# RWKV pairs: root transposes ahead of the increments, turned keys and a piece of weights between the states, the two decay products back to back

## The reference

```python
w = -softplus(-(w0 + tanh(wd) @ w2)) - 0.5
decay = exp(-exp(w))
a = sigmoid(a0 + ad @ a2)
kk = kk / max(sqrt(sum(kk * kk)), 1e-12)
k = k * (1.0 + (a - 1.0) * k_a)
aa = -kk
bb = kk * a4
def step(state, inp):
    sa = einsum('bhij,bhj->bhi', state, a_t)
    state = state * w_t + sa * b_t + v_t * k_t
    return state, einsum('bhij,bhj->bhi', state, r_t)
y = (y - mean) * rsqrt(var + RWKV_GN_EPS) * ln_w + ln_b
```

## Time and profile before

| | |
|---|---|
| median of three runs | 3329.46 us (3325.09 to 3331.16) |
| profiled execution | 3329.62 us |
| its span | 3327.8 us |
| PE busy | 3242.5 us, 97% of the span |
| PE weight loads busy | 2664.4 us, 80% |
| DVE, ACT, POOL busy | 53%, 37%, 6% |
| DMA | 97 GB/s on average |

### The profile page before, as it was taken

One profiled execution on the slowest core, in us unless ns is written; L12 is line 12 of the kernel. 1 busy time (PEld: TensorE's weight loads), 2 busy tenths in 40 slices (PEclk: granted clock), 3 DMA queues, 4 the chain that ended last, 5 costly groups with the idle time before them and its releaser, 6 DMA issues. The chain is left out here.

```text
span 3327.8 us, 52710 instructions
## 1 busy us (share of the span) xinstructions
PE 3242.5 (97%) x22179; PEld 2664.4 (80%) x22179; DVE 1774.2 (53%) x2970; ACT 1247.7 (37%) x1967; POOL 193.2 (6%) x156
## 2 busy tenths in 40 slices
PE   7999999999999999989999999999999999999999
PEld 6877777777777787867788888888888888888887
DVE  5235555545555455363436777433656566655832
ACT  4124343433333332242325666323334344443421
POOL 1000000001001111100000111010000000000000
PEclk9999999999999999999999999999999999999999
DMA  7433333331212134332442122443332233322552
GB/s 234 114 82 87 86 98 92 87 109 48 62 54 83 57 113 146 95 114 76 111 110 80 45 58 86 130 145 108 89 89 89 76 95 94 96 89 76 165 143 85
DMA packets 492528, 324.30 MB, mean 97 GB/s; under 512 B 27130, under 2 KB 448605, under 8 KB 491782
## 3 DMA queue, kind: packets, MB, share of 16 engines
q1 hardware_dynamic: 492294, 320.94, 33.3%
HBM read 276.05 MB, written 44.85 MB: 96 GB/s over the span
## 5 line engine op out<-in xcount | busy, mean ns | idle before, releaser
L534 PE MATMUL PS<-XH,WHT 128*128 128x512 f32 (+1 forms) x2224 | 897.7, 404 | 7.1 <-DVE AR L1031 2.1
L522 DVE TENSOR_TENSOR WLT<-AR,WHT 128x1024 fp32r<-128x1024 f32 (+1 forms) x430 | 527.3, 1231 | 667.2 <-ACT WHT L516 666.8
L536 PE MATMUL PS<-XH,WLT 128*128 128x512 f32 (+1 forms) x2224 | 872.6, 392 | 0.0
L516 ACT ACTIVATE WHT<-AR 128x1024 fp32r<-128x1024 f32 (+1 forms) x430 | 446.9, 1042 | 646.6 <-PE PS L536 483.5
L535 PE MATMUL PS<-XL,WHT 128*128 128x512 f32 (+1 forms) x1712 | 671.2, 392 | 0.0
L534 PEld LDWEIGHTS PS<-XH,WHT 128*128 128x128 f32 (+1 forms) x2224 | 417.5, 188 | 109.2 <-issue 10.8
L536 PEld LDWEIGHTS PS<-XH,WLT 128*128 128x128 f32 (+1 forms) x2224 | 417.7, 188 | 96.2
L535 PE MATMUL PS<-ARR,WHT 128*128 128x512 f32 x1024 | 404.6, 395 | 0.0
L535 PEld LDWEIGHTS PS<-XL,WHT 128*128 128x128 f32 (+1 forms) x1712 | 321.7, 188 | 71.7 <-issue 4.6
L535 PEld LDWEIGHTS PS<-ARR,WHT 128*128 128x128 f32 x1024 | 192.4, 188 | 40.4 <-issue 0.2
L534 PE MATMUL PS<-XL,WHT 128*128 128x512 f32 x512 | 203.3, 397 | 0.1
(11 more groups left out here) (487 smaller groups left out, 5336.5 us busy)
## 6 DMA issues: line engine op xcount, KB each, us to landing
AR<-b_w_in SPq DMA_DIRECT2D x128, 512.0 KB, 4.0
AR<-w_in SPq DMA_DIRECT2D x122, 512.0 KB, 4.1
AR<-a_w_in SPq DMA_DIRECT2D x48, 512.0 KB, 4.4
AR<-w_out SPq DMA_DIRECT2D x32, 512.0 KB, 4.8
AR<-a_w_out SPq DMA_DIRECT2D x32, 512.0 KB, 4.0
AR<-b_w_out SPq DMA_DIRECT2D x32, 512.0 KB, 4.1
proj_scratch<-AR SPq DMA_DIRECT2D x33, 256.0 KB, 2.0
AR<-a_w_kv_up SPq DMA_DIRECT2D x32, 256.0 KB, 3.7
```

The source lines that it names most:

```text
L516: self.nc.scalar.activation(self.shaped(self.high, n), self.shaped(self.raw, n), ACT.Copy).then_inc(self.s_high, 1)
L522: self.nc.vector.tensor_tensor(self.shaped(self.low, n), self.shaped(self.raw, n), f32(self.shaped(self.high, n)), ALU.subtract).then_inc( ...
L534: mm(out, wh, xh[k0 + c], start=(start and c == 0), stop=False)
L536: last = mm(out, wl, xh[k0 + c], start=False, stop=(stop and c == nk - 1))
```

## The change

Nothing is added or taken from the arithmetic. (1) The two decay products stand next to each other after level 2, the second into bank 7. (2) In the tail of PE, the root transposes come before the increments, the first state before the products of y, piece 7 and the turned keys between states. (3) ACT writes rb first and does its high split of weights after the exponentials. (4) DVE does kn, yn and the rates before the state inputs, hb and qt are apart, and the low split comes last.

```diff
@@ -1415,19 +1415,20 @@
                 else:
-                    N.wait(pe, i, "act.sgw")
-                N.did(mm(B[6][:, :], W2[rows(e), :], TW[rows(e), :], start=True, stop=True), "pe", ("zw", "za")[e])
+                    E.wait(pe, i - 2, "act.yc")
+                    N.wait(pe, i - 1, "dve.bon")
+                N.did(mm(B[6 + e][:, :], W2[rows(e), :], TW[rows(e), :], start=True, stop=True), "pe", ("zw", "za")[e])
...
             def key_sums(i):
                 N.wait(pe, i, "act.sqk")
                 if i:
-                    N.wait(pe, i, "act.sga")
+                    N.wait(pe, i, "act.sgw")
...
             def key_roots(i):
-                N.wait(pe, i, "act.rb")
+                N.wait(pe, i, "act.rb", "act.sga")
@@ -1494,6 +1495,8 @@
             def value_scores(i):
                 N.wait(pe, i, "act.tokV")
                 N.wait(pe, i, "dve.bon")
+                if i + 1 < NPAIR:
+                    N.wait(pe, i + 1, "act.sga")
@@ -1569,8 +1574,8 @@
             ahead(1)
             decays(0, 0)
+            decays(0, 1)
             ahead(2)
-            decays(0, 1)
@@ -1603,33 +1608,36 @@
-                    if l in (2, 3) and more:
-                        decays(i + 1, l - 2)
+                    if l == 2 and more:
+                        decays(i + 1, 0)
+                        decays(i + 1, 1)
...
                 solved(i)
                 piece(i, 6)
-                increments(i)
-                outputs(i)
-                state(i, 1)
+                if more:
+                    key_roots(i + 1)
                 if tail:
                     out_roots(i - 1)
-                if more:
-                    key_roots(i + 1)
+                increments(i)
+                queries_solved(i)
+                state(i, 1)
+                outputs(i)
                 state(i, 2)
                 if more:
                     values_turned(i + 1)
                 state(i, 3)
+                piece(i, 7)
                 state(i, 4)
                 if more:
                     bs_turned(i + 1)
                 state(i, 5)
-                state(i, 6)
-                piece(i, 7)
                 if more:
                     ks_turned(i + 1)
+                state(i, 6)
+                if more:
                     as_turned(i + 1)
                 from_state(i)
@@ -1791,12 +1799,14 @@
-                split(i, 3)
+                if more:
+                    spread(i + 1)
                 if tail:
                     out_spread(i - 1)
                 if more:
-                    spread(i + 1)
                     exps(i + 1)
+                split(i, 3)
+                if more:
                     token_major(i + 1, V_, "V")
@@ -2041,34 +2058,40 @@
                     key_recip(i + 1)
                     scan(i + 1)
-                state_inputs(i)
-                split(i, 3)
-                state(i, 1)
-                if tail:
-                    out_normed(i - 1)
-                state(i, 2)
                 if more:
                     unit_keys(i + 1)
                 if tail:
-                    out_bonus(i - 1)
-                state(i, 3)
+                    out_normed(i - 1)
                 if more:
                     rates(i + 1)
-                state(i, 4)
+                state_inputs(i)
+                if more:
+                    decayed_rates(i + 1)
+                bare_states(i)
+                if tail:
+                    out_bonus(i - 1)
+                state(i, 1)
                 if tail:
                     out_gated(i - 1)
                 if more:
                     scaled_keys(i + 1)
+                state(i, 2)
+                if more:
+                    decayed_keys(i + 1)
+                state(i, 3)
+                if more:
+                    removals(i + 1)
+                state(i, 4)
+                state_queries(i)
+                if more:
+                    queries(i + 1)
                 state(i, 5)
                 if more:
-                    decayed_keys(i + 1)
-                    removals(i + 1)
+                    bonus(i + 1)
                 state(i, 6)
-                if more:
-                    queries(i + 1)
-                    bonus(i + 1)
                 if tail:
                     low(i - 1)
+                split(i, 3)
                 evac(tile(i, 1))
```

More of the change, by code:

```diff
@@ L1221, in rwkv @@
               pool=[f"lot{l}" for l in levels],
-              pe=[f"{x}{h}{l}" for l in levels[:-1] for x in "xt" for h in halves] + ["uv"] + [f"{x}{h}{NL - 1}" for x in "xt" for h in halves] + ["pt0", "pt1", "gt0", "h0", "gt1", "h1", "q", "y"] + [f"s{c}" for c in range(1, NCH - 1)] + ["yf"],
+              pe=[f"{x}{h}{l}" for l in levels[:-1] for x in "xt" for h in halves] + ["uv"] + [f"{x}{h}{NL - 1}" for x in "xt" for h in halves] + ["pt0", "pt1", "gt0", "h0", "gt1", "h1", "q", "s1", "y"] + [f"s{c}" for c in range(2, NCH - 1)] + ["yf"],
               act=[f"xc{h}{l}" for l in levels for h in halves] + ["uvc", "ptc0", "ptc1"],
-              dve=[f"ta{h}{l}" for l in levels for h in halves] + ["gti", "hb", "qt"] + [f"su{c}" for c in range(1, NCH - 1)])
+              dve=[f"ta{h}{l}" for l in levels for h in halves] + ["gti", "hb"] + [f"su{c}" for c in range(1, 5)] + ["qt"] + [f"su{c}" for c in range(5, NCH - 1)])
     E = Marks(k, "rwkvy", pe=["cen", "var", "vt"], act=["yy", "sqy", "yc", "vsqrt", "vb", "xh"], dve=["ve", "vrec", "yn", "yb", "yz", "xl"])
@@ L1519, in increments, with queries_solved @@
                     S.did(both(cs, one), "pe", f"h{h}")
+            def queries_solved(i):
+                S.did(each(range(NCH), lambda c, e: mm(B[0][rows(e), tok(c)], P1TA[rows(e), c, 1, :], GB[rows(e), c, 1, :], start=True, stop=True)), "pe", "q")
             def outputs(i):
-                S.did(each(range(NCH), lambda c, e: mm(B[0][rows(e), tok(c)], P1TA[rows(e), c, 1, :], GB[rows(e), c, 1, :], start=True, stop=True)), "pe", "q")
                 E.wait(pe, i - 1, "dve.ve")
@@ L1662, in gates @@
                     N.wait(act, i, "pe.za")
-                    N.did(A(AS, B[6][:, :], ACT.Sigmoid, bias=k.prm("a0", i)), "act", "sga")
+                    N.did(A(AS, B[7][:, :], ACT.Sigmoid, bias=k.prm("a0", i)), "act", "sga")
             def split(i, j):
@@ L1869, in rates, with decayed_rates @@
                 N.did(TTn(SQN, KK, AS, ALU.mult), "dve", "ba")
+            def decayed_rates(i):
                 N.wait(dve, i, "dve.ba", "act.ewi")
@@ L1932, in state_inputs, with bare_states @@
                 S.did(TTn(GTI, B[2][:, :].rearrange("p (c f) -> p c f", f=CH), eye(NCH), ALU.add), "dve", "gti")
+            def bare_states(i):
                 S.wait(dve, i, "pe.h1")
@@ L1936, in state_inputs, with state_queries @@
                 S.did(TTn(HB, B[3][:, :].rearrange("p (c f) -> p c f", f=CH), WC2[i % 2].unsqueeze(2).broadcast_to([P, NCH, CH]), ALU.mult), "dve", "hb")
+            def state_queries(i):
                 S.wait(dve, i, "pe.q")
@@ L2006, in _ @@
             rates(0)
+            decayed_rates(0)
             scaled_keys(0)
```

## The result

The changed kernel takes 3297.08 us (median of four runs, 3295.54 to 3298.23); the kernel before, run on the same chip beside it, 3330.31 (3325.09 to 3338.04). The ratio is 0.9898 with an interval of 0.9878 to 0.9918: about 33 us less by the medians. The profiled execution took 3298.23 with a span of 3296.4, which is 31.4 less than the span before. Forecast were 3304.5, 25.15 us less, in a range from 3297 to 3314. The direction and the place are right, the size is too small.

A forecast was written before the change was run, and what follows sets the result against it. PE, busy 97% of the span, was taken as the bound, with open waits in the pairs' tails. 17.4 + 3.4 + 1.1 - 0.8 + 2.85 + 1.2 = 25.15 us from 3329.62 gave 3304.5 us, range 3297 to 3314.

The forecast's parts named there:

- the tail's four waits on PE: Tails of pairs 0 to 5: waits before turned values, fourth state, turned b and sixth state, 2.93 us together, would go.
- the new one: Tail, ahead of the first state: PE would newly wait 0.34 us for hb, which waits for bt on DVE.
- The decays: Ahead of level 3: two decay products side by side take 1.05 to 1.1 us; pairs 1 to 5 keep 0.26 each.
- the decays aren't staggered: Rival at the decay products: staggered, about 1.6 us, total 3308.7; 8 in 100 together with the serial case, 3313.
- DVE doesn't bound the tail: Rival in the tail: DVE becomes its bound, each pair loses 1 to 2 us, 3310 to 3316; 9 in 100.
- rb isn't late: Slower rival: key roots wait for a late rb and hold up all behind; with 4.6 us, 3336; 2 in 100.
- the size of the tail: Tails of pairs 0 to 5: each would gain 2.9 us, 17.4 us over six pairs.
- The step-by-step clock of the prediction: Tail of pair 2, timed step by step from differences of successive starts: `from_state` at 931.05 instead of 933.96.
- a third of its slow stretch: Tail of pair 6: half clock would last 6.8 us instead of 10.2, giving back 1.2 of 3.5 us lost.
- the two ends named: Pair 6: one slow stretch more or less (2.3 to 3.5 us), its 1.5 us of unexplained wait gone or not.
- The 0.8 us that the forecast takes off for it: Pair 7: out roots hold up increments for 1.3 us, hb costs 0.35, y gives 0.8 back: -0.8 us.
- The term itself: Levels and prologue, from the decay products: 5 x 0.26 + 2 x 1.05 = 3.4 us.

The follow-up runs named there:

- decays_undone: Changed kernel with the decay products put back, one ahead of level 3 and one ahead of level 4, in one bank: 3298.98 us, ratio 0.9903.
- decays_alone: Kernel before with only the two decay products side by side after level 2, in two banks: 3327.99 us, ratio 0.9984.
- evac_first: Changed kernel with DVE's evacuation of the projection's bank at level 3 ahead of the two steps mixing the keys: 3290.02 us, ratio 0.9878.
- piece7_old: Changed kernel with piece 7 and the turned keys back at their old place, piece 7 behind the sixth state: 3307.84 us, ratio 0.9919.
- best: Changed kernel with evacuation first except in pair 6, hb ahead of bt, and increments ahead of the roots in pairs 6 and 7: 3288.21 us, ratio 0.986.
- roots_behind: Changed kernel with the roots behind the first state on PE, and gti, hb and the first addition ahead of kn on DVE: 3304.38 us, ratio 0.9908.
- before_again: The kernel before, unchanged, profiled once more in one execution: 3337.49 us.
- back_later: Kernel before with pair 6's 1 MB transfer of `XL` issued after the products of y: 3329.36 us, ratio 0.9997.
- both best ones: `best`, and the same kernel with pair 6's first megabyte transfer started after the products of y: 3288.45 us, ratio 0.9855 for the latter.

## What of the prediction held, and the steps that failed

**What held.** What bounds the kernel: the tail's four waits on PE. All four are gone, and the new one is there, 0.30 us for 0.34. `decays_undone` shows that the reordered tails alone give nearly everything. Rb comes in time in pairs 0 to 5. Put_bonus and the Gram products don't slip: the Gram products of two pairs wait 0.83 us as before. The decays: a pair of them in 1.06 us; 0.26 us kept per pair, the rest a wait ahead of piece 4 (0.72 for some 0.8), shown by `decays_alone`, and its cause, the order on DVE, by `evac_first`. Pairs 6 and 7 wait 1.20 us for the roots (forecast 1.25 and 1.3), and pair 6 0.39 ahead of its fourth state. The tail of pair 5 is at full clock, worth 2.9 us for 2.85. Of the rivals none came: the decays aren't staggered, DVE doesn't bound the tail, and rb isn't late.

Which of the moves in the tail fills which wait is shown in part. Piece 7 between the states is worth 1.6 us a pair (`piece7_old`), hb ahead of bt another 0.27 (`best`), and the roots' place ahead of the increments nothing that can be seen (`roots_behind`). That the waits ahead of the turned values and the turned b went because DVE does kn and the rates earlier follows from the rows; no run puts these steps of DVE, or ACT's order, back alone.

**The step that failed: the size of the tail.** "It is the 2.93 of the waits, less 0.34, and some 0.3": 2.9 us a pair. Measured are 3.6. The brackets that make up the 2.93 begin at the modelled end of the work before, and that lies later than the time at which PE could have gone on. By successive starts the four intervals were 1.46 (second state to values turned), 0.69 (third to fourth state), 1.37 (fourth state to b turned) and 0.69 (fifth to sixth state), 4.21 us. Behind the same four states the next work now starts after 0.12, 0.21, 0.16 and 0.11, 0.60 in all. So the waits were worth 3.61, not 2.93, 0.17 more for each. Less the 0.30 that are new, 3.3 remain; roots and piece 6 are 0.07 shorter each, and the first and the sixth state, next to other work than before, 0.15 together.

The step-by-step clock of the prediction has the same fault from the other side: it put 0.21 to 0.25 for a state, read off a place where 128-row work follows. In the row a state now takes 0.11 to 0.16 where 64-row work follows, five times, and 0.21 ahead of piece 7. The Trainium skill, "Perfetto Trace Analysis", section "Summary: the profiler window per engine type", says that TensorE's records have an estimated end; the trace agrees, with the 0.17 us. `piece7_old` shows it independently: 1.32 us of brackets, 1.6 us of tail. Over six pairs this is 4 us of the 6 that were missed.

**The second step: pair 6.** Forecast were 1.1 for the waits and 1.2 for a third of its slow stretch; the tail gave 6.7. By the executions this splits up: `before_again`, at full clock and with 0.98 of stall, has 19.41, so with the 1.51 of the profiled one it would be 19.94, and its slow stretch cost 3.2 us. All of it went. The stall went too, 1.5 us; PE comes to that place later now, as it waits 1.20 us for the roots first, and the block of code (told at the end) is in by then. The remaining 2.0 are the waits, where 1.1 was forecast: the 3.6 of the other pairs, less the new 1.20 and 0.39. That I left this pair a slow stretch and the stall was the wrong choice between the two ends named.

**Pair 7.** The 0.8 us that the forecast takes off for it are there: from `solved` to `from_state` it takes 13.32 us for 12.52. But the profile of before has a slow stretch of 3.4 us right behind, at 1252.2, and that of the changed kernel has none there; the part from `from_state` on is 1.5 us shorter by it. All four profiles with the old tails have a stretch at this place, and two of the six with filled ones. Whether the change had a part in it is open, and the forecast had no term for it.

**What was taken back.** Levels and prologue gave 1.4 us in place of 3.4. The term itself holds: pairs 1, 3, 4 and 5 have -0.23 to -0.28, pair 6 -1.0, the prologue 1.2 by the key sums. But the two slow stretches of 3.4 us in the windows above cost some 2.6 together (against them stands 0.45 that pair 2 of the profiled kernel before took longer than its neighbours). Neither can be laid to the change alone. In the prologue `before_again` and `decays_undone` have a stretch of 6.8 us at the same place, all eight profiles with both decays together one of 3.4, and the first profile of the kernel before and `back_later` none. The one in pair 2 follows the new 0.72 us in both profiles of the changed kernel, one follows it in pair 5 of `piece7_old`, and none in `decays_alone` and `roots_behind`, which have that wait in five pairs each. `decays_undone` and `evac_first`, without it, have none in the levels.

**How far one profile carries.** The kernel before spreads from 3324.8 to 3338.4 us over 23 runs on one chip, the changed one over 3 and 5 us in four runs each, but `evac_first` and `best`, with tails filled as well, over 8 and 11. The four profiles with the old tails (the kernel before twice, `back_later`, `decays_alone`) show three to five of eight tails at half clock for 3.4 to 10.2 us, in other pairs each time but for pairs 5 and 7, and each costs 1.4 to 3.2. In the six profiles with filled tails (the changed one twice, `decays_undone`, `evac_first`, both best ones) none of pairs 0 to 6 has one in its tail. So filling the waits was worth more than their length. That the waits, and not something that goes with them, let the clock fall is only borne out by these ten. `piece7_old` speaks against waits as such: it puts two of them back in each of pairs 0 to 6, 0.39 and 0.93 us, and none of its tails is at half clock. Which waits it takes stays open.

## What to carry to other kernels

Price a wait on TensorE by the difference of successive starts with and without it, not by its bracket: here each of four waits was worth some 0.17 us more than it showed. Where short products with waits between them sit beside stretches at half clock, count the stretches over several profiles before you decide what filling the waits is worth, as they move from run to run. And when work moves up, see what the bank it needs hangs on: here two operations in front of an evacuation took back 0.8 of 1.05 us in each of five pairs, and turning them round gave 5 us in the rows, 7 by the medians, which are of two chips. See too what covers each step in the pairs that lack a piece of work: an order on DVE that cost nothing in six pairs cost PE 2.84 us in the seventh.

## What the runs showed of the hardware

- **Half clock after little waiting.** In the old tails, where PE waits 0.38 to 1.14 us at four places between products of 64 rows, the granted clock fell to 0.50 in three to five of eight tails per profile. In `piece7_old`, with 0.39 and 0.93 us per tail, it fell in none. In pair 2 of the changed kernel it fell right behind a single wait of 0.72 us, in both of its profiles.
- **A wait for code.** PE stopped for 0.90 to 1.59 us in pair 6 in four profiles (the kernel before twice, `decays_alone`, `best`), each time until 1.3 to 1.5 us after a 16 KB block of the queue "instruction" landed. The block came in at the end of SP's 1 MB transfer into `XL` and landed 0.3 to 0.9 us after the last of it. With the transfer issued later the stop is gone in both kernels that tried it (the kernel before and the best one). The Trainium skill, "Runtime: NRT & Kernel Launch", section "Instruction fetch mechanics", says that engines load their program in blocks of 16 KiB on a queue of their own, and that this is mostly hidden; the trace agrees on the blocks, and here it isn't hidden. That PE waits for just this block follows from the times and the two runs; no view names it.
- **Two heads side by side.** Two products of 64 rows, 128 columns and 512 tokens on the two halves of the rows, two records each, take 1.06 us together and 1.05 alone. The single records start in twos, at 882.27 and 882.28 us and at 882.80 and 882.81, and end in that order. The Trainium skill's strict order of starts and ends, as the prediction read it (both records of the first product ahead of the last of the second), would have given 1.6, and that didn't come. The four records as such are in order of start and end; they don't say which product each belongs to.
